# An expert's high and low rows stacked on 128 partitions for one combine product, and routing in one pass over five blocks of logits

## The chip, the cores and the metric

The kernel runs on one core of a Trainium2 chip. The metric is device time in microseconds (us). TensorE (PE) multiplies, VectorE (DVE), ScalarE (ACT) and GpSimd (POOL) work on elements, and SyncE (SP) issues most of the transfers between device memory and the on-chip memory of 128 partitions. PSUM is the memory of eight banks that TensorE writes to.

## The reference

One layer of a flow-matching backbone for 384 tokens (128 of context and 256 latent) of width 1024, in float32. The first half is a token mixer: modulation, an input projection, a bidirectional recurrence and a Fourier mixer, an output projection and a layer norm. The change lies in the second half, a hierarchical mixture of experts:

```python
pg = softmax(t @ wg + bg)                       # 4 expert groups
g = argmax(pg); p_top = pg[g]
le = (t @ we + be).reshape(ntok, 4, 4)          # 4 experts in each group
pe = softmax(le[g]); v, idx = top_k(pe, 2); v = v / sum(v)
w_k = p_top * v
eidx = g * 4 + idx
comb = sum(one_hot(eidx, 16) * w_k)             # 384 x 16
hid = silu(t @ w_gate[e]) * (t @ w_up[e]) * comb[:, e]
out = sum over e of hid @ w_down[e]             # each expert: 1024 -> 512 -> 1024
x = layer_norm(alpha * x + g2 * out)
```

Every token goes to two experts of one group, so there are 768 rows of work over 16 experts.

## The kernel before

Tokens lie in three tiles of 128 (`NT`). The routing turns the logits (`lg`, for each token 4 of groups, then 16 of experts) into marks and positions. `first_max` is a helper of five steps on VectorE. Each waits for the one before it (`link`), and together they take a maximum over the last axis, mark where it is reached, and reduce the marks to the first one. It runs over the group logits, then over the experts of each of the four groups, then once more with the first experts pushed down, for the second choice. Masks by the chosen group follow, then a scan that ranks the tokens. From the ranks TensorE computes each row's place among 768 slots, while VectorE makes the low part of tile 1 (`low_part(1)`) of the split tokens. `pick` and `pick2` mark the slots (`sel`), and the dispatch products (L1731) move the tokens' high and low parts (`h2H`, `h2L`) into slot order. Meanwhile come the gate weights (`comb`).

Then the experts run one after another, 48 weight units of 2 MB (gate, up and down for each of 16) streaming through a ring of seven buffers. SyncE issues unit v in order, and from the eighth on waits for unit v-7 to be used:

```python
                else:
                    sp.wait_ge(s["unit_used"], v - SLOTS + 1)
                sp.dma_start(weights(v, D if j == 2 else 512), experts[j][:, e]).then_inc(ring_in[v % SLOTS], 16)
```

Each engine's program is forked by the number of rows of the expert. `few` is for at most 64 rows (`HALF`) and `many` for up to 128. In this data experts 0 and 2 go through `many` and the others through `few`. With few rows the two 512-column halves of the expert's output lie on partitions 0 to 63 and 64 to 127 of one PSUM bank (L1830). ScalarE rounds this output to `yh` (`y_out`), VectorE subtracts to get the rest, `yl` (`y_low`), and TensorE multiplies both parts with the marks `selT` (`combine`), three times, once for each token tile. With few rows `selT` holds the same marks on both halves of the partitions. VectorE's `gather` weighs the product with the gate and adds it to the output (L1212).

TensorE's order is written out by hand. The combine of an expert is spread between the products of the next two:

```python
            for e in range(LAST - 1):
                project_in(e + 1, 0)
                if e:
                    combine(e - 1, 0)
...
                turn(e)
...
                project_in(e + 1, 1)
                if e:
                    combine(e - 1, 1)
...
                project_out(e)
                if e:
                    combine(e - 1, 2)
```

At e = 13 four `g2_row` products (L1925) that broadcast the last gate are put between these. After the loop come `turn(14)`, `combine(13, 0)`, `slot_weights` (L1915), `combine(13, 1)`, the output of expert 14, and the gate product of expert 15. Expert 15's output goes another way (`combine_last`), added to the residual that GpSimd (L1443, L1444) and VectorE (`settle`) prepare, and then the layer norm is taken.

Of the kernel before, what the change touches and what calls it, by code (L numbers as in the profile page):

```python
# [7 lines left out]
F32 = mybir.dt.float32  # L8
# [3 lines left out]
ALU = mybir.AluOpType  # L12
# [3 lines left out]
P = 128  # L16
# [5 lines left out]
NT = TOK // P  # L22
# [90 lines left out]
def build(nc, t):  # L113

    ctx = ExitStack()
    with ctx:
# [3 lines left out]
        def at(name, off, shape, dt=F32):  # L120
            return nc.alloc_sbuf_tensor_at(name, shape, dt, offset=off)
# [10 lines left out]
        def keep(name, shape, dt=F32):  # L132
# [36 lines left out]
        rt = keep("rt", [P, 8, NT, NE])  # L169
        stq = at("stq", place[0], [P, 24])  # L170
# [82 lines left out]
            "unit_used xs_ready sg_done silu_done hid_done ht_ps hts_done yh_done yl_done selA2 selT_done "  # L253
# [137 lines left out]
        def y_parts(e):  # L391
            return yh, yl
# [66 lines left out]
        def _(act):  # L459
# [200 lines left out]
            for n in range(2 * KD):  # L660
                if n == KD // 2:
                    act.wait_ge(s["prow_ps"], 1)
                    act.copy(Prow[:, :, :], PS[:, 0:2, 0:TOK]).then_inc(s["prow_sb"], 1)
                    act.wait_ge(s["x1_done"], NT)
                x_out(n)
                if n == KD + 1:
                    act.wait_ge(s["gap_done"], 1)
                    act.activation(rt[:, 6, :, 0:NG], rt[:, 5, :, 0:NG], ACT.Exp).then_inc(s["pos_pool"], 1)
                    act.activation(rs[:, 5, :], rs[:, 4, :], ACT.Exp).then_inc(s["pos_pool"], 1)
# [47 lines left out]
            def y_out(e):  # L717

                used(act, unit(e, 2))
                if e < LAST:  # L720
                    need(act, "c_ps", NT * e)
                need(act, "yl_done", e)
                if e == 0:
                    act.wait_ge(s["disp_sb"], 2 * KD)
                dst = y_parts(e)[0]
                fork(act, counts[e],
                     lambda: act.copy(dst[:, 0:512], PS[:, 3, :]).then_inc(s["yh_done"], 1),  # L727
                     lambda: act.copy(dst[:, :], PS[:, 3:5, :].rearrange("p a n -> p (a n)")).then_inc(s["yh_done"], 1))
# [49 lines left out]
        def _(dve):  # L778
# [277 lines left out]
            def by_group(v):  # L1056
                return v.rearrange("p i (g e) -> p i g e", e=EPG)

            og, oh1, oh2, asg = rt[:, 0, :, 0:NG], rt[:, 1], rt[:, 2], marks16[:, :, :]
            mx1, mx2, top = rt[:, 3, :, 0:NG], rt[:, 3, :, NG:2 * NG], rt[:, 3, :, 2 * NG:3 * NG]  # L1060
# [11 lines left out]
            link(dve.tensor_tensor_scan(rt[:, 7].rearrange("p i e -> p (i e)"), cst[:, C_SEG:C_SEG + NT * NE],  # L1072
                                        rt[:, 4].rearrange("p i e -> p (i e)"), 0.0, ALU.mult, ALU.add))
            dve.tensor_tensor(before16[:, :, :], rt[:, 7], rt[:, 4], ALU.subtract).then_inc(s["assign_done"], 1)
# [4 lines left out]
            place_ps = PS[:, 0, 0:NT * NE].rearrange("p (i e) -> p i e", e=NE)  # L1079
            step(dve.tensor_tensor(rt[:, 7], place_ps, oh1, ALU.mult))  # L1080
            step(dve.tensor_tensor(rt[:, 4], place_ps, oh2, ALU.mult))
# [3 lines left out]
            step(dve.tensor_reduce(pw[:, 1, :], rt[:, 4], AX.X, ALU.add))  # L1085
# [45 lines left out]
            step(dve.tensor_tensor(rt[:, 5, :, 0:NG], gl, wide(rs[:, 0, :], NG), ALU.subtract))  # L1131
            link(dve.tensor_tensor(rt[:, 4, :, 0:NG], mx2, mx1, ALU.subtract))
            link(dve.tensor_tensor(rt[:, 4, :, 0:NG], rt[:, 4, :, 0:NG], og, ALU.mult))
            link(dve.tensor_reduce(rs[:, 4, :], rt[:, 4, :, 0:NG], AX.X, ALU.add))
# [5 lines left out]
            link(dve.tensor_reduce(rs[:, 6, :], rt[:, 6, :, 0:NG], AX.X, ALU.add))  # L1140
            link(dve.tensor_scalar(rs[:, 7, :], rs[:, 5, :], 1.0, None, ALU.add))
            link(dve.tensor_tensor(rs[:, 6, :], rs[:, 6, :], rs[:, 7, :], ALU.mult))
            link(dve.reciprocal(wk[:, 0, :], rs[:, 6, :]))
            link(dve.tensor_tensor(wk[:, 1, :], wk[:, 0, :], rs[:, 5, :], ALU.mult))
            step(dve.tensor_tensor(rt[:, 3], oh1, wide(wk[:, 0, :], NE), ALU.mult))
            link(dve.tensor_tensor(rt[:, 4], oh2, wide(wk[:, 1, :], NE), ALU.mult))
            dve.tensor_tensor(comb[:, :, :], rt[:, 3], rt[:, 4], ALU.add).then_inc(s["comb_done"], 1)
# [46 lines left out]
            def y_low(e):  # L1194

                dve.wait_ge(s["yh_done"], e + 1)
                high, low = y_parts(e)
                fork(dve, counts[e],
                     lambda: dve.tensor_tensor(low[:, 0:512], PS[:, 3, :], high[:, 0:512].bitcast(F32), ALU.subtract)  # L1199
                     .then_inc(s["yl_done"], 1),  # L1200
                     lambda: dve.tensor_tensor(low[:, :], PS[:, 3:5, :].rearrange("p a n -> p (a n)"),
                                               high[:, :].bitcast(F32), ALU.subtract).then_inc(s["yl_done"], 1))
# [245 lines left out]
        def _(pe):  # L1448
# [368 lines left out]
            def project_out(e):  # L1817
# [3 lines left out]
                need(pe, "yh_done", e)  # L1821
# [21 lines left out]
            def combine(e, i):  # L1843

                if i == 0:
                    pe.wait_ge(s["yh_done"], e + 1)
                    pe.wait_ge(s["yl_done"], e + 1)
                    pe.wait_ge(s["selT_done"], e + 1)
# [6 lines left out]
                parts = y_parts(e)  # L1855

                def few():
                    for q, part in enumerate(parts):
                        for h in range(2):
                            mm = pe.matmul(PS[:, banks[h], :], m[HALF * h:HALF * (h + 1), i * P:(i + 1) * P],  # L1860
                                           part[HALF * h:HALF * (h + 1), 0:512], start=(q == 0), stop=(q == 1))
                    mm.then_inc(s["c_ps"], 1)

                def many():
                    for q, part in enumerate(parts):
# [168 lines left out]
```

## Time and profile before

| | us |
|---|---|
| median of 3 runs | 487.63 |
| lowest, highest | 487.33, 774.69 |
| profiled execution, its own time | 490.8 |
| its span | 488.6 |
| TensorE busy | 448.0 (92%) |
| VectorE busy | 236.4 (48%) |
| ScalarE busy | 121.7 (25%) |
| GpSimd busy | 63.3 (13%) |

The mean granted TensorE clock of that execution is 0.981 of full speed. It moved 146.90 MB, of which about 101 MB are expert weights. The span is from the first to the last instruction. The time is that of the whole execution, 2.2 us more. Busy time of one engine beside another is no cost in itself; what counts is which wait ends last at each place.

### The profile page before, as it was taken

How to read it: one execution, taken by the hardware profiler on the slowest of the kernel's cores; microseconds unless marked ns; L12 is line 12 of the kernel's file. 1: busy time of each engine (PE TensorE's matmuls, PEld its weight loads, DVE VectorE, ACT ScalarE, POOL GpSimd, SP SyncE). 2: the span in 40 equal slices, each digit the busy share in tenths (PEclk: the TensorE clock that was granted, in tenths of full speed). 3: DMA queues.
4: the chain of work that ended last, by engine and by line, in shares of the span. 5: the costliest groups of instructions: out<-in, count | busy, mean ns of one | idle time of the engine just before them, and what ended most of it. 6: DMA issues, size and time to landing. Idle time of an engine off the chain costs nothing.

```text
span 488.6 us, 6510 instructions
## 1 busy us (share of the span) xinstructions
PE 448.0 (92%) x2394; PEld 242.8 (50%) x2394; DVE 236.4 (48%) x446; ACT 121.7 (25%) x242; POOL 63.3 (13%) x61
## 2 busy tenths in 40 slices
PE   2679999999999999799999999999999999898882
PEld 1344455556554466696555444555554544363520
DVE  3552713848744257931024252444444445436767
ACT  2400168682220225162111111111111111121200
POOL 2000024357550430012000000000000000000300
PEclk9989999999999999799999999999999999999988
DMA  8999994855999026810899999999999999999403
GB/s 227 381 387 386 322 387 183 308 208 200 343 334 354 25 92 253 299 47 10 316 399 391 391 332 400 390 394 396 395 389 393 395 397 392 390 404 391 195 2 129
DMA packets 65380, 146.90 MB, mean 301 GB/s; under 512 B 3689, under 2 KB 4521, under 8 KB 65337
## 3 DMA queue, kind: packets, MB, share of 16 engines
q1 hardware_dynamic: 64144, 143.40, 80.1%
q10 hardware_dynamic: 1032, 2.81, 1.6%
q8 instruction: 29, 0.48, 0.4%
q0 software_dynamic: 160, 0.10, 0.3%
q14 instruction: 15, 0.11, 0.1%
HBM read 144.72 MB, written 1.58 MB: 299 GB/s over the span
## 4 chain that ended last, share of the span: by engine, by line
PE 71%; SPq 10%; DVE 6%; DMA 5%; issue 3%; ACT 2%; POOLq 1%; POOL 0%; DVEq 0%; ACTq 0%
PE PS L1790 18%; PE PS L1830 9%; PE PS L1656 8%; PE PS L1554 8%; PE PS L1797 6%; SPq L411 5%; PE PS L1860 4%; PE PS L1731 4%; DMA ring<-in_ex_w_gate 4%; SPq L416 2%; PE PS L1482 2%; PE PS L1531 2%; DMA dft<-in_dft 1%; PE PS L1837 1%; PE PS L1588 1%
## 5 line engine op out<-in xcount | busy, mean ns | idle before, releaser
L1790 PE MATMUL PS<-ring,xs 128*64 128x256 f32 x896 | 102.9, 382 | 2.3 <-DMA ring<-in_ex_w_gate 1.9
L1790 PEld LDWEIGHTS PS<-ring,xs 128*64 128x64 f32 x896 | 61.8, 137 | 39.3 <-issue 10.8
L1554 PE MATMUL PS<-hT,ring 128*128 128x388 f32 x192 | 67.5, 502 | 2.6 <-DVE hT L891 2.6
L1212 DVE SCALAR_TENSOR_TENSOR y<-PS,comb,y 128x1024 f32<-128x1024 f32 x42 | 53.6, 1278 | 0.4 <-PE PS L1867 0.3
L1554 PEld LDWEIGHTS PS<-hT,ring 128*128 128x128 f32 x192 | 36.7, 194 | 31.6 <-issue 8.3
L1830 PE MATMUL PS<-ring,hTs 128*64 128x512 f32 x224 | 51.2, 598 | 0.9 <-DMA ring<-in_ex_w_down 0.9
L1443 POOL TENSOR_TENSOR y<-y,g2r 128x1024 f32<-128x1024 f32 x1 | 2.4, 2362 | 236.1 <-DVE y L1212 236.1
L1830 PEld LDWEIGHTS PS<-ring,hTs 128*64 128x64 f32 x224 | 14.8, 136 | 30.9 <-issue 30.8
L727 ACT CAST yh<-PS 128x512 fp32r<-128x512 f32 x13 | 7.6, 586 | 88.9 <-PE PS L1830 56.7
L1199 DVE TENSOR_TENSOR yl<-PS,yh 128x512 fp32r<-128x512 f32 x13 | 9.0, 692 | 42.2 <-ACT yh L727 42.2
L1482 PE MATMUL PS<-ring,cond 128*32 128x512 f32 x192 | 25.0, 637 | 1.9 <-DVE cond L818 1.9
L1169 DVE SCALAR_TENSOR_TENSOR hid<-sg,PS 128x256 f32<-128x256 f32 x14 | 5.9, 421 | 37.8 <-PE PS L1790 37.8
L1656 PE MATMUL PS<-ring,yfs 128*128 128x512 f32 (+1 forms) x56 | 21.9, 533 | 0.0
L1656 PE MATMUL PS<-ring,mixT 128*128 128x512 f32 (+1 forms) x56 | 21.8, 531 | 0.0
L1400 POOL TENSOR_SCALAR gtmp<-gtmp 128x388 f32<-128x388 f32 x8 | 9.7, 1210 | 83.4 <-ACT gtmp L532 83.4
L1860 PE MATMUL PS<-yh,selT 64*128 64x512 f32 x78 | 19.3, 492 | 0.8 <-issue 0.8
L1731 PE MATMUL PS<-sel,h2H 128*128 128x384 f32 x48 | 18.1, 378 | 1.4 <-DVE sel L1100 1.4
L702 ACT ACTIVATE sg<-PS 128x256 f32<-128x256 f32 x14 | 5.4, 384 | 50.2 <-PE PS L1790 50.2
L1731 PE MATMUL PS<-sel,h2L 128*128 128x384 f32 x48 | 17.8, 370 | 0.0
L1860 PEld LDWEIGHTS PS<-yh,selT 64*128 64x128 f32 x78 | 7.3, 183 | 20.8 <-issue 20.7
L920 DVE TENSOR_SCALAR rtmp<-rtmp 128x388 f32<-128x388 f32 x8 | 6.2, 774 | 23.4 <-ACT rtmp L539 23.3
L1157 DVE SCALAR_TENSOR_TENSOR sg<-sg,PS 128x256 f32<-128x256 f32 x14 | 5.9, 422 | 21.8 <-ACT sg L702 21.8
(273 smaller groups left out, 606.1 us busy)
## 6 DMA issues: line engine op xcount, KB each, us to landing
ring<-in_ex_w_gate SPq DMA_DIRECT2D x16, 2048.0 KB, 14.1
ring<-in_ex_w_up SPq DMA_DIRECT2D x16, 2048.0 KB, 16.9
ring<-in_ex_w_down SPq DMA_DIRECT2D x16, 2048.0 KB, 15.0
ring<-in_w_ada SPq DMA_DIRECT2D x11, 2048.0 KB, 12.2
ring<-in_w_in SPq DMA_DIRECT2D x2, 2048.0 KB, 22.2
ring<-in_w_out SPq DMA_DIRECT2D x2, 2048.0 KB, 10.3
ring<-in_w_ada SPq DMA_DIRECT2D x2, 1024.0 KB, 15.2
ring<-in_w_in SPq DMA_DIRECT2D x2, 1024.0 KB, 14.7
```

The costliest lines, as they stand in the source:

```text
L411: sp.dma_start(dst[:, k0:, :], src[:, k0:, c0:c0 + 512]).then_inc(ring_in[(u + 1) % RING], 16)
L416: sp.dma_start(wbd[64 * h:64 * h + 64, 8 * gi:8 * gi + 8, 64 * h:64 * h + 64], t[n][0].rearrange("d (c q) i j -> q i (d c) j", q=2)[h]).th ...
L1212: dve.scalar_tensor_tensor(out=y, in0=src, scalar=comb[:, i, e:e + 1], in1=y, op0=ALU.mult, op1=ALU.add).then_inc(s["acc_done"], 1)
L1482: mm = pe.matmul(PS[32 * j:32 * j + 32, SUM_BANK[g], :], cond32[:, k, 6 - 2 * m:38 - 2 * m], w[:, k, :], start=(m == 0 and k < 4), stop=(l ...
L1531: mm = pe.matmul(PS[:, 4 + gi, 0:W], wbd[:, 8 * gi + 4 * d + c, :], xc[:, c, :], start=True, stop=True)
L1554: mm = pe.matmul(PS[:, w % 4, 0:W], wt[:, k, (w % 4) * P:(w % 4 + 1) * P], hT[:, k, :], start=(k == 0), stop=(k == KD - 1))
L1656: mm = pe.matmul(PS[:, bank, 0:nc_], x, unit3(ring[(WOUT_UNIT[h] + 1) % RING])[:, c, c0 % 512:c0 % 512 + nc_], start=(n == 0), stop=(n == ...
L1731: mm = pe.matmul(PS[:, 4 + n % 4, 0:HS], part[:, i, k * P:(k + 1) * P], sel[:, i, h * HS:(h + 1) * HS], start=(i == 0 and part is h2H), st ...
L1790: mm = pe.matmul(PS[HALF * h:HALF * (h + 1), bank, 0:FE // 2], x(k, HALF), w[:, k, h * (FE // 2):(h + 1) * (FE // 2)], start=(k == 0), sto ...
L1797: mm = pe.matmul(PS[:, bank, :], x(k, CAP), w[:, k, :], start=(k == 0), stop=(k == KD - 1))
L1830: mm = pe.matmul(PS[HALF * h:HALF * (h + 1), 3, :], x, w[:, f, h * 512:(h + 1) * 512], start=(f == 0), stop=(f == KF - 1))
L1860: mm = pe.matmul(PS[:, banks[h], :], m[HALF * h:HALF * (h + 1), i * P:(i + 1) * P], part[HALF * h:HALF * (h + 1), 0:512], start=(q == 0), ...
```

## The change

For an expert with at most 64 rows, the high parts of both output halves and their low parts go into one tile `yh` of 128 partitions by 1024. In the columns of half h, the high part stays on partitions 64h to 64h+63, and the low part goes to the other 64. ScalarE makes two copies of 64 partitions and VectorE two subtractions that read one half of the partitions and write the other. The combine product then takes the whole of `selT`'s 128 partitions, whose two halves are the same marks, and yields high plus low at once: two matmuls for each token tile where there were four. Nothing changes for an expert with more rows. The semaphore `yh_done` becomes `yh_part`, which counts two for each expert.

The routing runs `first_max` once over five blocks of four logits (the group block and the four expert blocks), and once over the four blocks for the second choice. The masks by the chosen group are applied to the sum of both marks first. Those of `oh1` and `oh2` alone come after the counts have been handed to TensorE. Tiles for the gate weights move, with the same number of steps.

```diff
-            first_max(gl, C_COD4, og, rs[:, 0, :], rt[:, 5, :, 0:NG], rs[:, 11, :])
-            x4, oh14, oh24, tmp4 = by_group(rt[:, 7]), by_group(oh1), by_group(oh2), by_group(rt[:, 4])
-            first_max(by_group(el), C_COD4, oh14, mx1, tmp4, top)
-            link(dve.scalar_tensor_tensor(out=rt[:, 7], in0=oh1, scalar=-2e30, in1=el, op0=ALU.mult, op1=ALU.add))
-            first_max(x4, C_COD4, oh24, mx2, tmp4, top)
+            first_max(by_group(lg[:, :, :]), C_COD4, by_group(oh5[:, :, :]), mx5, by_group(mark5[:, :, :]), top5[:, 1])
+            link(dve.scalar_tensor_tensor(out=rt[:, 7], in0=first, scalar=-2e30, in1=el, op0=ALU.mult, op1=ALU.add))
+            first_max(by_group(rt[:, 7]), C_COD4, by_group(oh2), mx2, by_group(rt[:, 4]), top)
             og4 = og.unsqueeze(3).broadcast_to([P, NT, NG, EPG])
-            step(dve.tensor_tensor(oh14, oh14, og4, ALU.mult))
-            link(dve.tensor_tensor(oh24, oh24, og4, ALU.mult))
-            dve.tensor_tensor(asg, oh1, oh2, ALU.add).then_inc(s["assign_done"], 1)
-            link(dve.tensor_tensor(rt[:, 4], oh1, oh2, ALU.add))
+            link(dve.tensor_tensor(pair, first, oh2, ALU.add))
+            dve.tensor_tensor(by_group(asg), by_group(pair), og4, ALU.mult).then_inc(s["assign_done"], 1)
+            link(dve.tensor_tensor(by_group(pair), by_group(pair), og4, ALU.mult))
...
+            step(dve.tensor_tensor(by_group(oh1), by_group(first), og4, ALU.mult))
+            step(dve.tensor_tensor(by_group(oh2), by_group(oh2), og4, ALU.mult))
             low_part(1)
...
+                def few():
+                    for h in range(2):
+                        act.copy(yh[half_rows(h), 512 * h:512 * (h + 1)], PS[half_rows(h), 3, :]).then_inc(s["yh_part"], 1)
...
+                def few():
+                    for h in range(2):
+                        dve.wait_ge(s["yh_part"], 2 * e + h + 1)
+                        low = dve.tensor_tensor(yh[half_rows(1 - h), 512 * h:512 * (h + 1)], PS[half_rows(h), 3, :],
+                                                yh[half_rows(h), 512 * h:512 * (h + 1)].bitcast(F32), ALU.subtract)
+                    low.then_inc(s["yl_done"], 1)
...
                 def few():
-                    for q, part in enumerate(parts):
-                        for h in range(2):
-                            mm = pe.matmul(PS[:, banks[h], :], m[HALF * h:HALF * (h + 1), i * P:(i + 1) * P],
-                                           part[HALF * h:HALF * (h + 1), 0:512], start=(q == 0), stop=(q == 1))
+                    for h in range(2):
+                        mm = pe.matmul(PS[:, banks[h], :], m[:, i * P:(i + 1) * P], yh[:, 512 * h:512 * (h + 1)],
+                                       start=True, stop=True)
                     mm.then_inc(s["c_ps"], 1)
```

## Rows read from the trace of the kernel before

**Rows 1.** The page, the span in 40 slices: transfer rate of each slice.

```profile
GB/s 227 381 387 386 322 387 183 308 208 200 343 334 354 25 92 253 299 47 10 316 399 391 391 332 400 390 394 396 395 389 393 395 397 392 390 404 391 195 2 129
```

**Rows 2.** Timeline of SyncE's queue, expert stage: start us, us, line, what.

```profile
230.42 0.37 SPq L432 DMA_DIRECT2D ring<-in_ex_w_down  x1
...
289.84 0.37 SPq L432 DMA_DIRECT2D ring<-in_ex_w_up  x1
...
368.47 5.32 SPq L432 DMA_DIRECT2D ring<-in_ex_w_down  x1
...
425.08 1.09 SPq L432 DMA_DIRECT2D ring<-in_ex_w_gate  x1
```

**Rows 3.** Timeline of TensorE, 420 to 457.5 us: the last wait for weights, expert 15.

```profile
426.59 3.67 PE L1790 MATMUL PS<-ring,xs 128*64 128x256 f32 x32 [0.93 <-DMA ring<-in_ex_w_gate]
...
452.40 3.67 PE L1790 MATMUL PS<-ring,xs 128*64 128x256 f32 x32
```

**Rows 4.** Transfer issues from 425 us to 426.1 us: KB, us to landing.

```profile
ring<-in_ex_w_gate SPq DMA_DIRECT2D x1, 2048.0 KB, 22.2
```

**Rows 5.** Timeline of VectorE, the routing: start us, us, line, what.

```profile
193.40 0.17 DVE L1046 TENSOR_REDUCE rs<-lg 128x3 f32<-128x12 f32 x1
...
194.42 0.20 DVE L1046 TENSOR_REDUCE rt<-lg 128x12 f32<-128x48 f32 x1
...
197.07 0.21 DVE L1067 TENSOR_TENSOR rt<-rt 128x48 f32<-128x48 f32 x1
...
197.79 0.26 DVE L1072 TENSOR_TENSOR_SCAN rt<-cst,rt 128x48 f32<-128x48 f32 x1
...
198.21 1.22 DVE L1020 TENSOR_TENSOR h2L<-PS,h2H 128x1024 fp32r<-128x1024 f32 x1
```

**Rows 6.** Timeline around the dispatch, and the chain's piece of its last 42.

```profile
201.55 0.66 PE L1731 MATMUL PS<-sel,h2H 128*128 128x384 f32 x1 [1.44 <-DVE sel L1100]
...
204.76 0.62 DVE L1100 SCALAR_TENSOR_TENSOR sel<-cst,pw,selA 128x384 fp32r<-128x384 f32 x1
...
208.57 1.50 PE L1746 MATMUL PS<-cst,pw 128*128 128x128 f32 x12
...
216.22 7.31 PE PS L1731 x42
```

**Rows 7.** Windows: us, busy of each engine, PEclk (granted clock), DMA share, GB/s.

```profile
202.00:204.00 2.00, 2.00 (x8) 2.00 (x8) 1.96 (x4) 0.00 (x0) 0.00 (x0) 0.50 0.90 294
```

**Rows 8.** Timeline of TensorE: a combine of expert 2 (many), two of expert 14.

```profile
311.97 0.73 PE L1867 MATMUL PS<-yh,selT 128*128 128x512 f32 x2
...
313.10 3.65 PE L1830 MATMUL PS<-ring,hTs 128*64 128x512 f32 x16
...
456.00 0.50 PE L1860 MATMUL PS<-yh,selT 64*128 64x512 f32 x2
456.34 0.39 PE L1860 MATMUL PS<-yl,selT 64*128 64x512 f32 x2
...
456.80 0.40 PE L1860 MATMUL PS<-yl,selT 64*128 64x512 f32 x2
457.13 3.67 PE L1790 MATMUL PS<-ring,xs 128*64 128x256 f32 x32
```

**Rows 9.** Timeline of all engines from 455 us: where the chain leaves TensorE.

```profile
456.93 0.42 DVE L1157 SCALAR_TENSOR_TENSOR sg<-sg,PS 128x256 f32<-128x256 f32 x1 [0.51 <-ACT sg L702]
...
458.73 2.36 POOL L1443 TENSOR_TENSOR y<-y,g2r 128x1024 f32<-128x1024 f32 x1 [236.06 <-DVE y L1212]
```

**Rows 10.** Timeline at expert 13's output: copy, subtraction, gather, combine.

```profile
443.76 0.59 ACT L727 CAST yh<-PS 128x512 fp32r<-128x512 f32 x1 [3.88 <-PE PS L1860]
...
444.59 0.69 DVE L1199 TENSOR_TENSOR yl<-PS,yh 128x512 fp32r<-128x512 f32 x1 [4.22 <-ACT yh L727]
...
445.20 1.27 DVE L1212 SCALAR_TENSOR_TENSOR y<-PS,comb,y 128x1024 f32<-128x1024 f32 x1
...
445.65 0.50 PE L1860 MATMUL PS<-yh,selT 64*128 64x512 f32 x2 [0.84 <-issue]
```

More of the change, by code:

```diff
@@ L169, in build @@
         rt = keep("rt", [P, 8, NT, NE])
+        oh5 = at("oh5", router0, [P, NT, NG + NE])
+        mark5 = at("mark5", router0 + 256, [P, NT, NG + NE])
+        top5 = at("top5", router0 + 512, [P, 2, NT, 5])
         stq = at("stq", place[0], [P, 24])
@@ L389, in halves, with half_rows @@
             return v.rearrange("p (a n) -> p a n", n=512)
-        def y_parts(e):
-            return yh, yl
+        def half_rows(h):
+            return slice(HALF * h, HALF * (h + 1))
         @block.sync
@@ L1064, in _ @@
-            link(dve.scalar_tensor_tensor(out=rt[:, 7], in0=oh1, scalar=-2e30, in1=el, op0=ALU.mult, op1=ALU.add))
-            first_max(x4, C_COD4, oh24, mx2, tmp4, top)
+            mx5 = top5[:, 0]
+            first_max(by_group(lg[:, :, :]), C_COD4, by_group(oh5[:, :, :]), mx5, by_group(mark5[:, :, :]), top5[:, 1])
+            mx0, mx1 = mx5[:, :, 0], mx5[:, :, 1:]
+            og, first = oh5[:, :, 0:NG], oh5[:, :, NG:]
+            oh1, oh2, pair, asg = rt[:, 4], rt[:, 5], rt[:, 6], marks16[:, :, :]
@@ L1084, in _ @@
             step(dve.tensor_reduce(pw[:, 0, :], rt[:, 7], AX.X, ALU.add))
-            step(dve.tensor_reduce(pw[:, 1, :], rt[:, 4], AX.X, ALU.add))
+            step(dve.tensor_reduce(pw[:, 1, :], rt[:, 6], AX.X, ALU.add))
             dve.wait_ge(s["dve_step"], n_step[0])
@@ L1129, in _ @@
                 dve.tensor_scalar(io[:, q, :], io[:, q, :], -1.0, None, ALU.add).then_inc(s["io_done"], 1)
[L1131 to L1134, printed above, removed]
+            gaps, over, gap = mark5[:, :, 0:NG], mark5[:, :, NG:2 * NG], rs[:, 8, :]
+            step(dve.tensor_tensor(over, gl, wide(mx0, NG), ALU.subtract))
+            link(dve.tensor_tensor(gaps, mx2, mx1, ALU.subtract))
+            link(dve.tensor_tensor(gaps, gaps, og, ALU.mult))
+            link(dve.tensor_reduce(gap, gaps, AX.X, ALU.add))
             dve.nop().then_inc(s["gap_done"], 1)
@@ L1139, in _ @@
             dve.wait_ge(s["pos_pool"], 2)
[L1140 to L1147, printed above, removed]
+            total, ratio = rs[:, 10, :], rs[:, 9, :]
+            link(dve.tensor_reduce(total, mark5[:, :, 2 * NG:3 * NG], AX.X, ALU.add))
+            link(dve.tensor_scalar(rs[:, 11, :], ratio, 1.0, None, ALU.add))
+            link(dve.tensor_tensor(total, total, rs[:, 11, :], ALU.mult))
+            link(dve.reciprocal(wk[:, 0, :], total))
+            link(dve.tensor_tensor(wk[:, 1, :], wk[:, 0, :], ratio, ALU.mult))
+            step(dve.tensor_tensor(rt[:, 6], oh1, wide(wk[:, 0, :], NE), ALU.mult))
+            link(dve.tensor_tensor(rt[:, 7], oh2, wide(wk[:, 1, :], NE), ALU.mult))
+            dve.tensor_tensor(comb[:, :, :], rt[:, 6], rt[:, 7], ALU.add).then_inc(s["comb_done"], 1)
             counts = {}
@@ L1194, in y_low, with many @@
             def y_low(e):
[L1196 to L1202, printed above, removed]
+                def few():
[4 more added lines that the diff above has]
+                    low.then_inc(s["yl_done"], 1)
+                def many():
+                    dve.wait_ge(s["yh_part"], 2 * e + 2)
+                    dve.tensor_tensor(yl[:, :], PS[:, 3:5, :].rearrange("p a n -> p (a n)"),
+                                      yh[:, :].bitcast(F32), ALU.subtract).then_inc(s["yl_done"], 1)
+                fork(dve, counts[e], few, many)
             def gather(e, i):
@@ L1820, in project_out @@
                 pe.wait_ge(s["hts_done"], e + 1)
-                need(pe, "yh_done", e)
+                need(pe, "yh_part", 2 * e)
                 need(pe, "yl_done", e)
@@ L1854, in combine @@
                 banks = c_banks(e, i)
-                parts = y_parts(e)
                 def few():
-                    for q, part in enumerate(parts):
-                        for h in range(2):
-                            mm = pe.matmul(PS[:, banks[h], :], m[HALF * h:HALF * (h + 1), i * P:(i + 1) * P],
-                                           part[HALF * h:HALF * (h + 1), 0:512], start=(q == 0), stop=(q == 1))
+                    for h in range(2):
+                        mm = pe.matmul(PS[:, banks[h], :], m[:, i * P:(i + 1) * P], yh[:, 512 * h:512 * (h + 1)],
+                                       start=True, stop=True)
                     mm.then_inc(s["c_ps"], 1)
                 def many():
-                    for q, part in enumerate(parts):
+                    for q, part in enumerate((yh, yl)):
                         for h in range(2):
```

25 lines of the change are left out of this document (12 added, 13 removed).

## The prediction

> **What bounds the kernel now.** I first read the clock and the transfer rate by slice, then SyncE's queue, then TensorE's order of work, and last the three places that the diff touches.
>
> The expert stage, from about 223 us to 460 us, has two bounds that take turns. The transfer rate stands near 390 to 400 GB/s in nearly every slice from 232 us on, after two slices at 47 and 10 [rows 1]. The quiet comes because all seven buffers hold weights. SyncE can issue a load only when TensorE gives one back, the first at 230.42 [rows 2]. At first TensorE sets the pace: SyncE's issues are short (0.37 us) at 230.42 and at 289.84. Later the loads do: an issue at 368.47 takes 5.32 us, for the queue behind it is full [rows 2]. At 426.59 TensorE, which has worked through its lead, waits 0.93 us for gate weights [rows 3]. After that it is the bound again. It also makes the broadcast rows of the last gate there, and gate weights issued at 425.08 land 22.2 us later, at 447.3, and are used at 452.40, with 5.1 us to spare [rows 2 to 4]. From there on the chain runs through TensorE's short products, at 457.3 through VectorE into GpSimd [rows 9], and on to the last layer norm.
>
> So time saved on TensorE between 290 us and 426 us becomes a longer wait for loads. Only two things move the end: an earlier start of the expert stage, which moves the whole stream of loads, and what happens after 426.59.
>
> **Part 1, the combine product.** An expert with at most 64 rows takes four matmuls of 64 rows by 512 columns for each token tile now, and two of 128 rows afterwards. Half the instructions looks like half the time, but the rows say otherwise. The two matmuls of a pair, one on partitions 0 to 63 and one on 64 to 127, occupy 0.50 us together at 456.00, while two full ones in a row take 0.73 at 311.97 [rows 8]. The halves of the array therefore work side by side. From 456.00 to 457.13 stand two combine steps, that is four such pairs, in 1.13 us. From 311.97 to 313.10 stand four full matmuls, and they also take 1.13 us [rows 8]. A pair costs what one full matmul costs. The new step has two full matmuls for two pairs. Its entry is 0.34 (456.00 to 456.34) and its exit 0.33 (456.80 to 457.13), so it takes 0.67 us, against 0.66 now [rows 8]. I take a saving of 0. One bound is the inner step: 456.34 to 456.80 is two pairs, 0.23 each [rows 8]. If the exit fell to that, the saving would be 0.10 a step, at six steps on the chain after 426.59 (experts 12 and 13, three tiles each) 0.6 us. The other bound is a loss of 0.01 a step.
>
> The Trainium skill has the rule that speaks against this half of the change. "TensorEngine Tiling (Array Packing)", section "Theoretical Speedup", gives up to twice the throughput to products whose dimension is at most 64, since the array then works as two tiles. By that rule the kernel before already has the factor of two that stacking seems to bring, and the sum would hold nothing for it. The trace agrees, with 0.50 us for a pair. Without that rule the sum would hold six times 0.33 us, which is the second case below.
>
> **Part 2, making the stacked rows.** One ScalarE copy of 128 partitions by 512 (0.59 us at 443.76) becomes two of 64 partitions, and one VectorE subtraction (0.69 us, but 0.61 to the next start: 444.59 to 445.20) becomes two, the second after the second copy [rows 10]. No row has a 64-partition copy of this kind. Between half and all of the old duration each, I take all, since the number of elements per partition stays 512. The second copy runs beside the first subtraction, so the pair adds one subtraction, 0.61 us, before the low part is ready (bounds 0 and 0.69).
>
> For experts 1 and 3 to 12 a whole input product of 3.6 us lies between the expert's output and its combine, and it covers this. If it didn't, the load queue would still hide it. For expert 13 nothing covers it: ScalarE at 443.76, VectorE at 444.59, TensorE's combine at 445.65 after 0.84 us idle [rows 10]. There all of 0.61 lands on the chain. Behind it TensorE has the slot weights and the next output product, and VectorE its gathers, and all move with it. Expert 14's low part feeds a combine that has room, but VectorE serves it in order ahead of expert 15's gate product, before which VectorE idles 0.51 us at 456.93 [rows 9]. Of the second 0.61 about 0.10 is left over, and GpSimd's step at 458.73 waits for VectorE's gather right behind [rows 9]. ScalarE's later copies of gate rows slip 0.5 us under the same 0.61. Sum of part 2: +0.7 us.
>
> **Part 3, routing.** VectorE works alone here. The pass over the group logits, 193.40 to 194.42, is five linked steps of 0.20 us and goes (-1.02). Its five blocks now ride in the expert pass. Twelve elements cost 0.20 a step and 48 cost 0.24 (194.42 to 197.07, eleven steps), so 60 cost about 0.25, +0.07 over five steps [rows 5]. The four masks and sums from 197.07 to 197.79 (0.72) become three (0.24 + 0.12 + 0.24 = 0.60): -0.12. Two unlinked masks are made before the low part of tile 1, which started at 198.21, +0.24 [rows 5]. Sum: -0.83 us until the positions are ready. TensorE's ranks, which need only the first three terms, start 1.07 us earlier and stay ahead of VectorE, so nothing new is late. The renamed tiles for the gate weights keep their number of steps and lie under the dispatch.
>
> Dispatch then starts at 200.7 instead of 201.55 [rows 6]. Not all of this arrives. TensorE's granted clock is at its low level (1.2 GHz, 0.50 in the row) from 202 to 204 [rows 7]; before 201.55 it had idled 1.44 us for the marks [rows 6]. The first 24 dispatch matmuls take 7.02 us (201.55 to 208.57), where 42 later ones take 7.31 in all, 0.174 each [rows 6]. If the low stretch ends at the same instant as now, work done 0.83 us earlier is done at half speed and gives 0.42. If it moves with the work, it gives all 0.83. No row decides, and I take 0.6. Whatever arrives moves the first returned buffer at 230.42 and the whole stream of loads, hence the wait at 426.59.
>
> **The sum.** The profiled execution took 490.8 us, with 2.2 us outside its span of 488.6. Combine 0.0, stacked rows +0.7, routing -0.6: 490.9 us for the same conditions. The median of the runs shown is 487.63, 3.2 us below the profiled execution, so I forecast 487.7.
>
> **The rivals.** (a) The sum holds: within about 1 us of before, 487.7. For it: equal times for four pairs and four full matmuls. (b) The combine does become half as long, because the overlap of a pair is less real than the recorded ends say: six steps of 0.33 us after 426.59, -2.0, so 485.7. Against it, the start of the next product after each step is recorded too, and it shows 0.66. (c) Dispatch runs at the high level, because TensorE's gap before the ranks closes. Then the marks of the third tile set the pace. Their second VectorE step starts at 204.76 and takes 0.62 [rows 6], so they come 0.83 us earlier, at 204.55, and eight matmuls of 0.174 end at 205.9 rather than 208.57. This gives 2.6 us at the start in place of 0.6, and 485.7. For it, the idle gap shrinks; against it, the gap right before dispatch (the marks' own) is left as it is. (d) Slower: the subtraction that reads one half of the partitions and writes the other costs twice as much. Nothing in the trace writes across halves. It is priced at one more 0.69 at expert 13 and one more at expert 14, +1.4, and it decides as soon as both late low parts are more than 0.5 us above my price. With routing giving only 0.42 it comes to 489.3. That the change saves nothing at all on TensorE is no case of its own, it is part of (a).
>
> **How the numbers follow.** (a) 0.70, (b) 0.06, (c) 0.14, (d) 0.10. The range takes in the bounds of (a) (combine -0.6, stacked rows 0 to 0.8, routing 0.4 to 0.8, so 486.0 to 488.1), (b) and (c) at 485.7, and (d) at 489.3. The profiled execution's distance of 3.2 us from the median says that a median can itself sit a us or two elsewhere, so the range is 484.7 to 489.7. Two per cent, about what a measurement of this kernel can tell from no change, is 9.8 us, further than any case reaches: faster 0.02, within 0.96, slower 0.02.
>
> **What would show it.** In the changed kernel two matmuls per combine step with the next product 0.66 us after the first, whereas 0.33 would prove (b). VectorE from the first maximum to the low part of tile 1 in 4.0 us instead of 4.8. Two subtractions of about 0.7 us per expert, and TensorE idle some 0.6 us longer before expert 13's combine. Waits for weights of the same or greater length up to 427 us, at a wall clock 0.4 to 0.8 us earlier. The prediction is wrong if the wait for loads disappears, if the dispatch shows another clock, or if cross-half subtractions are dearer.

## The result, and the profile after

The changed kernel takes 484.9 us (median of 20 runs, 482.19 to 490.3) beside 488.15 us for the kernel before (20 runs). The ratio is 0.9928, 95% interval 0.9909 to 0.9947: 0.7% faster, about 3.3 us. The prediction had 487.7 us and no net gain. Ratios, and the means below, leave out a run that is more than 1.5% above the fastest of its kernel (774.69 us before, 490.3 us here, 494.36 us in e10_cost). The profiled execution took 485.24 us, with a span of 483.4 us against 488.6.

VectorE's timeline of the routing in the changed kernel (start us, us, line, what), which answers to [rows 5]:

```profile
192.12 0.22 DVE L1054 TENSOR_REDUCE top<-lg 128x15 f32<-128x60 f32 x1
...
196.08 1.22 DVE L1028 TENSOR_TENSOR h2L<-PS,h2H 128x1024 fp32r<-128x1024 f32 x1
```

From the first maximum to the low part of tile 1 it takes 3.96 us (192.12 to 196.08), where [rows 5] had 4.81: 0.85 less. Everything around 190 us also stands 1.3 us earlier in this execution, before any changed line has run (the last logit product starts at 191.43 instead of 192.71). That is variation between executions and not the change.

TensorE's timeline at the dispatch, for [rows 6], and a window (PEclk is the third value from the end), for [rows 7]:

```profile
196.08 0.17 PE L1730 MATMUL PS<-marks,tri_ones 128*128 128x16 bf16 x1 [0.32 <-DVE before L1081]
...
199.43 0.41 PE L1750 MATMUL PS<-sel,h2H 128*128 128x384 f32 x1 [1.68 <-DVE sel L1110]
...
203.82 1.50 PE L1765 MATMUL PS<-cst,pw 128*128 128x128 f32 x12
```

```profile
200.00:203.00 3.00, 3.00 (x19) 2.83 (x18) 2.93 (x6) 0.00 (x0) 0.00 (x0) 1.00 1.05 401
```

The gap ahead of the rank products is 0.32 us. The first 24 dispatch matmuls take 4.39 us (199.43 to 203.82) instead of 7.02, because the granted clock is 1.00 (2.4 GHz) where [rows 7] had 0.50 (1.2 GHz). This is the largest single difference between the two traces, 2.6 us. It is a difference between two executions, and it doesn't say how often each level occurs: the experiments come back to that. The trace of before holds a second low stretch, at the first product of the residual, which the changed kernel's trace doesn't have (TensorE's timeline, before and then changed):

```profile
463.58 3.66 PE L1902 MATMUL PS<-y,cst 128*128 128x512 f32 x4 [1.35 <-POOL y L1444]
```

```profile
460.04 1.98 PE L1919 MATMUL PS<-y,cst 128*128 128x512 f32 x4 [1.37 <-POOL y L1463]
```

TensorE's timeline in the expert stage of the changed kernel, for [rows 3, 8]:

```profile
383.69 0.73 PE L1877 MATMUL PS<-yh,selT 128*128 128x512 f32 x2 [0.38 <-DVE y L1231]
384.26 0.38 PE L1831 MATMUL PS<-cst,hid 128*128 128x128 f32 x2
...
388.17 0.74 PE L1877 MATMUL PS<-yh,selT 128*128 128x512 f32 x2
388.84 3.65 PE L1849 MATMUL PS<-ring,hTs 128*64 128x512 f32 x16
...
421.46 3.67 PE L1809 MATMUL PS<-ring,xs 128*64 128x256 f32 x32 [1.05 <-DMA ring<-in_ex_w_gate]
```

A combine step of two full matmuls takes 0.67 us to the start of an output product (388.17 to 388.84), as predicted, but 0.57 before a transpose (383.69 to 384.26), where the old form takes 0.66. And there is a wait that the prediction didn't have: 0.38 us for VectorE's gather. The waits of TensorE between 215 and 440 us (us in total, times, longest), first of the kernel before and then of the changed one:

```profile
PE PS L1790 <- DMA ring<-in_ex_w_gate: 1.9, 2, 1.0
PE PS L1830 <- DMA ring<-in_ex_w_down: 0.9, 1, 0.9
...
PE PS L1790 <- DMA ring<-in_ex_w_up: 0.4, 1, 0.4
```

```profile
PE PS L1877 <- DVE y L1231: 3.5, 9, 0.4
PE PS L1809 <- DMA ring<-in_ex_w_gate: 1.1, 1, 1.1
```

TensorE used to wait 3.2 us for loads. Now it waits 1.1 us for loads and 3.5 for VectorE. Expert 13 in the changed kernel (copies, subtractions, combine), for [rows 10], with what follows, and a window there:

```profile
438.24 1.19 ACT L731 CAST yh<-PS 64x512 fp32r<-64x512 f32 x2 [3.87 <-PE PS L1877]
...
438.85 1.39 DVE L1212 TENSOR_TENSOR yh<-PS,yh 64x512 fp32r<-64x512 f32 x2 [3.80 <-ACT yh L731]
...
440.61 0.74 PE L1877 MATMUL PS<-yh,selT 128*128 128x512 f32 x2 [1.51 <-issue]
...
443.13 5.13 PE L1849 MATMUL PS<-ring,hTs 128*64 128x512 f32 x16
```

```profile
443.00:446.00 3.00, 3.00 (x9) 1.01 (x10) 2.93 (x6) 0.00 (x0) 0.00 (x0) 0.50 1.06 401
```

The two subtractions take 1.39 us and TensorE idles 1.51 instead of 0.84, +0.67. In this execution the clock then falls to its low level, and the output product takes 5.13 us instead of 3.65.

### The profile page after: what moved, and what is told of

Its sections match the earlier page's. It is cut to its first block, busy times and chain, and to the rows that moved or that the text cites. A ratio compares the mean times of both kernels' runs of the same rounds, so it can differ in the third digit from the quotient of the medians.

```text
span 483.4 us, 6377 instructions
## 1 busy us (share of the span) xinstructions
PE 442.2 (91%) x2316; PEld 240.7 (50%) x2316; DVE 246.0 (51%) x455; ACT 129.1 (27%) x255; POOL 63.9 (13%) x61
## 4 chain that ended last, share of the span: by engine, by line
PE 77%; DVE 9%; DMA 6%; issue 5%; ACT 2%; SPq 1%; POOLq 1%; POOL 0%; DVEq 0%; ACTq 0%
PE PS L1809 17%; PE PS L1573 12%; PE PS L1849 9%; PE PS L1675 9%; PE PS L1816 6%; PE PS L1501 4%; DMA ring<-in_ex_w_gate 4%; PE PS L1877 4%; PE PS L1750 4%; PE PS L1550 2%; PE PS L1856 1%; DMA pos<-in_pos 1%; PE PS L1607 1%; PE PS L1884 1%; PE PS L1592 1%
## 5 line engine op out<-in xcount | busy, mean ns | idle before, releaser
L1849 PE MATMUL PS<-ring,hTs 128*64 128x512 f32 x224 | 52.6, 613 | 0.3 <-issue 0.3
L731 ACT CAST yh<-PS 64x512 fp32r<-64x512 f32 x26 | 15.1, 581 | 89.1 <-PE PS L1849 61.5
L1212 DVE TENSOR_TENSOR yh<-PS,yh 64x512 fp32r<-64x512 f32 x26 | 17.9, 689 | 40.2 <-ACT yh L731 40.0
L1877 PE MATMUL PS<-yh,selT 128*128 128x512 f32 x78 | 29.2, 458 | 5.0 <-DVE y L1231 3.5
L1877 PEld LDWEIGHTS PS<-yh,selT 128*128 128x128 f32 x78 | 11.9, 188 | 24.7 <-issue 24.6
L1750 PE MATMUL PS<-sel,h2H 128*128 128x384 f32 x48 | 16.5, 343 | 1.7 <-DVE sel L1110 1.7
L1006 DVE TENSOR_TENSOR tmp<-PS,rows 128x512 f32<-128x512 f32 (+1 forms) x7 | 4.3, 616 | 24.3 <-PE PS L1675 24.3
L1750 PE MATMUL PS<-sel,h2L 128*128 128x384 f32 x48 | 16.1, 335 | 0.0
```

The lines of the kernel that those rows point to most:

```text
L731: act.copy(yh[half_rows(h), 512 * h:512 * (h + 1)], PS[half_rows(h), 3, :]).then_inc(s["yh_part"], 1)
L1212: low = dve.tensor_tensor(yh[half_rows(1 - h), 512 * h:512 * (h + 1)], PS[half_rows(h), 3, :], yh[half_rows(h), 512 * h:512 * (h + 1)].bit ...
L1750: mm = pe.matmul(PS[:, 4 + n % 4, 0:HS], part[:, i, k * P:(k + 1) * P], sel[:, i, h * HS:(h + 1) * HS], start=(i == 0 and part is h2H), st ...
L1849: mm = pe.matmul(PS[HALF * h:HALF * (h + 1), 3, :], x, w[:, f, h * 512:(h + 1) * 512], start=(f == 0), stop=(f == KF - 1))
```

## The experiments

Each ran beside the kernel before on the same chip, in three batches. The mean granted clock of every execution is on record, so each kernel has a mean time and a mean clock over its runs. Of the kernel before, the 87 runs taken beside the experiments average 488.3 us and 0.9834. Of the changed one, 31 (first result and e4) average 484.8 us and 0.987. A mean clock doesn't say where in a run the low stretches lie. In the traces they are found at three places behind 34 us and ahead of 470 us: the dispatch, expert 14's output, and the first product of the residual.

| label | ratio to before, 95% interval | mean us | mean clock |
|---|---|---|---|
| e1_routing | 0.9956, 0.9928 to 0.9985 | 486.6 | 0.9865 |
| e2_combine | 0.9984, 0.9957 to 1.0011 | 487.4 | 0.9826 |
| e3_fill | 1.0047, 1.0022 to 1.0073 | 490.4 | 0.9866 |
| e4_after | 0.9928, 0.9900 to 0.9956 | 484.6 | 0.9873 |
| e5_fill2 | 0.9987, 0.9964 to 1.0010 | 486.9 | 0.9873 |
| e6_full | 0.9984, 0.9955 to 1.0013 | 487.2 | 0.9829 |
| e7_mixed | 0.9929, 0.9903 to 0.9956 | 484.6 | 0.9857 |
| e8_double | 1.0104, 1.0073 to 1.0134 | 493.0 | 0.9872 |
| e9_late | 1.0003, 0.9974 to 1.0033 | 488.1 | 0.9810 |
| e10_cost | 1.0062, 1.0030 to 1.0095 | 490.5 | 0.9809 |
| e11_best | 0.9922, 0.9892 to 0.9952 | 483.5 | 0.9887 |

My theory A after the result: the gain is routing's, through VectorE's time and through the clock of the dispatch, and the stacked rows cost 0.7 us. The rival B: the combine's halved matmuls.

**e1_routing, the routing half alone** (the diff is the first block of the change shown above).

> Only the routing half of the change; the combine is that of the kernel before. Theory A (the gain is routing's: 0.8 us less on VectorE ahead of the dispatch, and a dispatch whose granted clock is more often high, worth another 1 to 2.6 us; the stacked rows cost 0.7 us at expert 13): 3 to 4.5 us faster than before, 0.7 us faster than the whole change. Theory B (the gain is the combine's, half the matmuls on the chain after the last wait for weights): 0.5 to 1 us faster than before, slower than the whole change by 2.5 us.

It is 0.4% faster, about 2 us: less than A said and more than B said. The first 24 dispatch matmuls run at the high clock in its trace, and its mean clock is near that of the changed kernel, 0.9865. The same trace has low stretches at expert 14's output and at the residual.

**e2_combine, the stacked rows alone** (the other blocks).

> Only the stacked rows and the combine of two matmuls; the routing is that of the kernel before. Theory A: 0.3 to 1 us slower than before, with TensorE idle about 1.5 us instead of 0.84 before expert 13's first combine, and dispatch at whatever clock the kernel before has. Theory B: 2 to 3 us faster than before.

Against A, it isn't slower: 0.16% faster, with an interval that reaches over 1. Its clock is that of the kernel before. So B's 2 to 3 us isn't there, and neither is A's loss. The halves add up to most of the whole (1.7 and 0.9 us in the means, 3.5 for the whole).

**e3_fill, TensorE's gaps filled in the kernel before.**

```diff
+                for _ in range(count):
+                    pe.matmul(PS[:, 5, 0:64], ident, cst[:, C_ID:C_ID + 64], start=True, stop=True)
+
             pe.wait_ge(s["tri_done"], 1)
+            pe.wait_ge(s["x1_done"], NT)
+            busy(12)
             pe.wait_ge(s["assign_done"], 2)
...
             ada_sums(11, range(KD // 2, KD))
+            busy(16)
```

> The kernel before, with 12 small matmuls in TensorE's gap ahead of the rank products and 16 in its gap ahead of the dispatch; their results are not used. Theory A says that these gaps bring the granted clock down for the dispatch: with them filled, the first 24 dispatch matmuls take about 4.4 to 5.2 us instead of 7.0, and the time is about 1.5 to 2 us below that of the kernel before wherever that one had the low clock. If the clock has another cause, or isn't what costs time, no change within 0.5 us.

The filling was too long. Each call is two matmuls in the trace and costs 0.22 us, so the dispatch began 3.6 us late, and the kernel is slower, not faster as expected. Yet its 24 matmuls took 4.25 us and its mean clock rose to 0.9866, above the 0.9834 of the kernel before. That points to the gaps as what brings the clock down.

**e4_after, the changed kernel again.**

> The whole changed kernel once more, for a second trace and beside its halves: 3 to 4 us faster than before. By theory A its runs fall into groups by mean granted clock, a low stretch at the dispatch and one at expert 14's output being there or not, about 1.6 us of time for each 3.4 us at the low level; by theory B the clock of a run and its time are unrelated.

The same ratio as at first. In both sets the runs with a clock of 0.989 or 0.990 have spans near 481.6 us, those at 0.985 and 0.986 near 483.8, and those at 0.978 and 0.979 486.1. In its trace neither the dispatch nor expert 14's output is at the low level.

**e5_fill2, the same filling with 4 and 5 calls.**

> The kernel before with fewer small matmuls in TensorE's two gaps, 4 ahead of the rank products and 5 ahead of the dispatch, about 0.9 and 1.1 us; their results are not used. Dispatch should start 8.8 to 9.0 us after the last logit product, as in the kernel before, not 12.4 us as with the longer filling. Theory A (TensorE's gaps bring the clock down for the dispatch, and that is part of what routing gains): mean granted clock 0.986 or more instead of 0.983, and 1 to 1.5 us faster than before. If the clock isn't what costs time: no change within 0.5 us.

TensorE's timeline of e5_fill2 at the dispatch:

```profile
198.44 1.33 PE L1710 MATMUL PS<-cst 128*128 128x64 f32 x10
200.03 0.41 PE L1739 MATMUL PS<-sel,h2H 128*128 128x384 f32 x1 [0.26 <-DVE sel L1100]
...
204.45 0.72 PE L1754 MATMUL PS<-cst,pw 128*128 128x128 f32 x5
```

The dispatch starts 8.83 us after the last logit product, as before (8.84), and takes 4.42 us, where the trace of before had 7.02. The mean clock is 0.9873, and none of 12 runs is at or below 0.983, where 46 of 87 runs of the kernel before are. So the filling does raise the clock. The gain in time isn't shown: the interval reaches over 1. The mean is 1.3 us below the mean of all runs of before, and the medians of this comparison are 487.2 and 487.78.

**e6_full, two full matmuls on the old tiles.**

```diff
-                    for q, part in enumerate(parts):
-                        for h in range(2):
-                            mm = pe.matmul(PS[:, banks[h], :], m[HALF * h:HALF * (h + 1), i * P:(i + 1) * P],
-                                           part[HALF * h:HALF * (h + 1), 0:512], start=(q == 0), stop=(q == 1))
+                    for h, part in enumerate(parts):
+                        mm = pe.matmul(PS[:, banks[h], :], m[:, i * P:(i + 1) * P], part[:, 0:512], start=True, stop=True)
```

> The kernel before in all but the combine of an expert with few rows: two matmuls over 128 partitions, one on the high and one on the low tile, in place of four over 64. The output halves are mixed up by it, and ScalarE's copy and VectorE's subtraction stay single; so it has TensorE's side of the stacked rows without their cost. Theory A: about 1.5 us faster than before (0.3 outside the span, about 1.2 from shorter changes between tile shapes, mostly before the loads set the pace), with 0.84 us idle at expert 13 as before. If a full matmul costs what a pair costs and nothing else counts, as the prediction had it: no change within 0.5 us.

The mean is 1.1 us below before at the same clock (0.9829 and 0.9834), though the interval of the ratio reaches over 1. Its trace shows where TensorE's side saves. TensorE's timeline around expert 2 (its products use the whole array), first e6_full, then the kernel before:

```profile
270.23 7.03 PE L1797 MATMUL PS<-ring,xs 128*128 128x512 f32 x16
276.70 0.79 PE L1859 MATMUL PS<-yh,selT 128*128 128x512 f32 x1
...
277.66 3.65 PE L1830 MATMUL PS<-ring,hTs 128*64 128x512 f32 x16
```

```profile
274.27 7.03 PE L1797 MATMUL PS<-ring,xs 128*128 128x512 f32 x16
281.23 0.49 PE L1860 MATMUL PS<-yh,selT 64*128 64x512 f32 x2
...
281.89 3.65 PE L1830 MATMUL PS<-ring,hTs 128*64 128x512 f32 x16
```

From the start of the 16 matmuls to the next product it is 7.43 us instead of 7.62. Full-array products stand before and behind the first combine matmul, so the array doesn't change from one tile shape to another and back. Where the neighbours are split by columns, nothing is saved (281.24 to 281.91 is 0.67). From the gate product of expert 14 to the slot weights it takes 19.77 us instead of 20.32. The part outside the span stays at 2.14 us, not 1.83 as I had expected.

This trace and that of e10_cost show one more thing. Both kernels have the old routing and the old gaps, and yet the dispatch runs at the high level. TensorE's timeline of e10_cost:

```profile
196.59 0.17 PE L1716 MATMUL PS<-marks,tri_ones 128*128 128x16 bf16 x1 [1.39 <-DVE before L1074]
...
199.71 0.41 PE L1736 MATMUL PS<-sel,h2H 128*128 128x384 f32 x1 [1.45 <-DVE sel L1100]
...
204.10 1.50 PE L1751 MATMUL PS<-cst,pw 128*128 128x128 f32 x12
```

The first 24 matmuls take 4.39 us here and 4.42 us in e6_full. So the old gaps don't always bring a low stretch, and a single trace can't show that closing them removes it. Over many runs the difference is plain: 66 of 122 runs with the old routing (before, e2, e6, e10) have a mean clock of 0.983 or less, but 9 of 61 with the new one (changed, e1, e7, e8) and 1 of 24 with the old one and filled gaps (e3, e5).

**e7_mixed, the changed kernel with experts 13 and 14 in the old form.**

```diff
+        APART = (LAST - 2, LAST - 1)
...
                 def few():
+                    if e in APART:
+                        act.copy(yh[:, 0:512], PS[:, 3, :]).then_inc(s["yh_part"], 2)
+                        return
```

and the same fork in `y_low` and `combine`.

> The changed kernel, but experts 13 and 14 in the form before (one copy, one subtraction, four matmuls of 64 rows). TensorE's idle time before expert 13's first combine falls from 1.5 to 0.84 us. Theory A: 0.3 to 0.7 us faster than the changed kernel, since the load stream no longer covers these two experts. If the stacking costs nothing at expert 13: the same as the changed kernel within 0.3 us.

The trace has the gain: from the last wait for loads to the slot weights it takes 19.57 us, where e4_after takes 20.26. In this trace the dispatch is in part at the low level, with the new routing. The time doesn't show it clearly: 484.6 us in the mean, at a clock of 0.9857 against 0.987.

**e8_double, the suspected cost doubled.**

```diff
                         dve.wait_ge(s["yh_part"], 2 * e + h + 1)
+                        if h == 0:
+                            dve.tensor_tensor(yl[half_rows(0), 0:512], PS[half_rows(0), 3, :],
+                                              yh[half_rows(0), 0:512].bitcast(F32), ALU.subtract)
```

> The changed kernel with one more VectorE subtraction of 64 partitions by 512 for each expert with few rows, into a tile that isn't used: the suspected cost doubled. Theory A (for 11 of 13 experts the load stream covers it, and only expert 13 and a little of 14 pay): 0.6 to 1.3 us slower than the changed kernel. If it were paid by every expert: about 8 us slower.

Here A fell. The kernel is 8 us slower than the changed one: every expert pays. The waits of TensorE from 215 to 440 us in e8_double:

```profile
PE PS L1880 <- DVE y L1234: 11.1, 10, 1.4
```

No wait for loads is left. VectorE's subtraction stands ahead of the last gather of the expert before, that gather frees the PSUM banks of TensorE's next combine, and TensorE arrives at expert 14's gate weights 5 us after they have landed. What I had taken for cover, the stream of loads, was 3.2 us in all in the kernel before, and 1.1 us of it was left in the changed kernel.

**e9_late, VectorE's time put back into the routing.**

```diff
+            for _ in range(4):
+                link(dve.tensor_tensor(pair, first, oh2, ALU.add))
             link(dve.tensor_tensor(pair, first, oh2, ALU.add))
```

> The changed kernel with four more linked VectorE steps of 0.24 us ahead of the sum of the marks: 0.97 us put back into the routing, which also reopens TensorE's gap ahead of the rank products from 0.3 to about 1.3 us. If the gap matters for the clock (theory A): mean granted clock back from 0.987 to about 0.983, a low stretch at the dispatch in many executions, and 1.6 to 2.4 us slower than the changed kernel. If only VectorE's time counts: 1.0 us slower, with the same clock.

TensorE's timeline of e9_late at the ranks and the dispatch, and a window:

```profile
197.55 0.17 PE L1732 MATMUL PS<-marks,tri_ones 128*128 128x16 bf16 x1 [1.29 <-DVE before L1083]
...
201.00 0.41 PE L1752 MATMUL PS<-sel,h2H 128*128 128x384 f32 x1 [1.78 <-DVE sel L1112]
...
206.84 1.39 PE L1767 MATMUL PS<-cst,pw 128*128 128x128 f32 x11
```

```profile
202.50:205.50 3.00, 3.00 (x11) 3.00 (x11) 2.89 (x7) 0.00 (x0) 0.00 (x0) 0.50 0.99 332
```

The four steps add 1.07 us up to the dispatch (9.07 us after the last logit product instead of 8.00) and cost 3.3 us in all. The gap is open again, the dispatch is in part at the low level and takes 5.84 us, and the mean clock is 0.9810. The whole gain of the change is lost by four small instructions. This is the clearest evidence that time on this path is worth more than itself. Its trace also has a low stretch at expert 14's output, so not all of the lower mean clock need be the dispatch's.

**e10_cost, the kernel before with 0.6 us more on VectorE's path**: one more subtraction of 64 partitions by 512 for each expert with few rows.

> The kernel before with one more VectorE subtraction of 64 partitions by 512 for each expert with few rows, into columns that aren't used: the cost of the stacked rows without TensorE's side of them. By what the doubled cost showed, VectorE's delay is passed on to TensorE's first combine of every expert (about 0.4 us each, 9 or more times), which the load stream covers only up to the 3.3 us that TensorE waited for loads in the kernel before; so here the waits for loads shrink to about nothing, and the time grows by 0.7 (expert 13) to 2.0 us. If the load stream still covered all of it: 0.6 us. If nothing were covered: 5 us.

It is 0.62% slower, 2.2 us in the mean, a little over my 0.7 to 2.0, at a lower clock (0.9809 and 0.9834), so part of the 2.2 us may be the clock's. In its trace TensorE has no wait for loads left and 3.9 us of waits for VectorE's gather. As in e8_double, the cost is passed on, and the first 3.2 us of it go into waits that were there anyway.

**e11_best, the mixed kernel with fillings** (5 calls ahead of the dispatch, 5 ahead of the last residual product, as in e3_fill).

> The mixed kernel (changed, with experts 13 and 14 in the old form) with 5 small unused matmuls in TensorE's gap ahead of the dispatch and 5 in its gap ahead of the last residual product, to keep the clock. Theory A: mean granted clock 0.989 or more, no low stretch between 34 and 470 us in its trace, 0.5 to 1.5 us faster than the changed kernel, 4 to 5 us faster than before. If the fillings only delay the products behind them: the changed kernel's time or up to 0.5 us more.

It is the fastest: median 483.74 us, ratio 0.9922 (0.9892 to 0.9952). In the six runs the mean clock is 0.9887 and none is below 0.986. Its span in the trace is 480.2 us, with no low stretch between 34 and 470 us. Its advantage over the changed kernel, about 1.3 us in the means, lies inside the two intervals.

## Why the prediction was wrong

The forecast was a net +0.1 us, and the kernel became 3.3 us faster. Two terms of the sum were too small: routing, where the clock was priced as if the low stretch stayed, and the combine, taken as 0. The measured 484.9 us lies just inside the stated range, but only through the us or so that was added for the scatter of medians: the lowest case stood at 485.7. (By its own terms case (a) reaches down to 486.2 us, and not 486.0.) Two of the prediction's own signs of being wrong came: the dispatch shows another clock in the trace, and the waits for loads shrank from 3.2 to 1.1 us.

**The combine's bound by time (right in the main).** A full matmul does cost what a pair costs, and 0.67 us to the output product came as said. Rival (b), 0.33 a step, is refuted by the traces: four full matmuls in a row take 1.12 us in the changed kernel (452.45 to 453.57), as four pairs took 1.13 before [rows 8]. The rule that the prediction quoted from the Trainium skill, "TensorEngine Tiling (Array Packing)", section "Theoretical Speedup", agrees with the traces: the old form had its factor of two. The possible saving of 0.10 a step, which I named as a bound and took as 0, is real wherever the neighbour has the full shape: before transposes, before the gate-row products (437.25 to 437.82 is 0.57), and around expert 2. After the last wait for loads these came to about 0.7 us, and cancelled the stacked rows' cost there: from the gate product of expert 14 to the slot weights it takes 20.27 us, against 20.32 before and 19.77 in e6_full. Ahead of 290 us, where TensorE sets the pace of the loads, it returns buffers up to 0.5 us earlier. I had read the saving only on the chain's end and forgot my own first finding, that the start of the stage is TensorE's too. This term of the sum was mis-sized: 0.0 stood for about -1.1. That is the difference of means of e6_full, whose interval still reaches over 1; its trace supports it, with 0.5 us by 290 us and 0.55 behind the last wait for loads.

**Stacked rows (size right, reason wrong).** Expert 13 cost 0.67 us, predicted 0.61 and a rest of 0.10. For experts 1 and 3 to 12 the sentence that failed is that the input product "covers this". The wait of a combine for the banks of the gather before it stood in the code, with a margin of about 0.2 us, and I priced only the wait for the low part. It costs 3.5 us over nine experts. It shows nothing in the time because TensorE had 3.2 us of waits for loads to give, and the shape changes saved some more. That "the load queue would still hide it" held by luck, since I had not added these waits up. e8_double and e10_cost show that once they are used up, nothing more is covered.

**Routing on VectorE (right).** -0.83 predicted; in the trace -0.85 up to the low part of tile 1 and -0.84 up to the dispatch.

**The clock at the dispatch (the step that failed).** "If the low stretch ends at the same instant as now ... gives 0.42. If it moves with the work, it gives all 0.83. I take 0.6." Both assumed that the low stretch stays. Rival (c) had the right mechanism, that the gap before the ranks closes, and got 0.14. Its price was too low as well. It waited for the VectorE step at 204.76, but by the loop over `pick` and `pick2` that is the first tile's mark for the second half of the slots. The first 24 matmuls need the third tile's mark for the first half, one step earlier in VectorE's timeline of before:

```profile
203.77 0.62 DVE L1100 SCALAR_TENSOR_TENSOR sel<-cst,pw,selA 128x384 fp32r<-128x384 f32 x1
```

With it (c) comes to 3.6 us at the start, and the two traces differ by 3.47 us from the last logit product to the end of these matmuls. But all of this compares executions that have the low stretch with executions that haven't, and the kernel before itself has both kinds. What the change shifts is how often. The gap goes from 1.40 to 0.32 us (the one behind it grows from 1.44 to 1.68). The dispatch has a low stretch in one of the five traces with the new routing as it is (e7_mixed), and in two of the four with the old one (before and e2_combine, not e6_full and e10_cost). That is too few to tell. The mean clocks over many runs do tell, though not of the dispatch alone: 0.9834 to 0.987, back to 0.9810 with the gap reopened (e9_late), up to 0.9873 with it filled (e5_fill2). Within one kernel the span changes by 300 to 460 us per unit of mean clock (the kernel before 487.6 us at 0.978 and 485.1 at 0.986; the changed one 486.1 at 0.979 and 481.5 at 0.989), so a rise of 0.0033 is worth 1.0 to 1.5 us, an estimate.

**The sum as measured.** VectorE -0.85, clock -1.0 to -1.5, TensorE's side of the combine -1.1, expert 13 +0.7, and -0.31 us outside the span (2.14 us in the kernel before, about 1.83 in every kernel with stacked rows). That is -2.6 to -3.1 us, against -3.3 (medians) to -3.5 (means) measured. The rest is within the intervals. The 0.31 us is open. It isn't the number of TensorE's matmuls, since e6_full has as few and keeps 2.14. The clock's worth was tested only with its cause, never alone at equal times on every engine, so its size remains an estimate.

The two traces shown differ by more, 5.2 us of span, and this can be placed. 1.28 us lie ahead of the changed lines, 0.84 are VectorE's, and 2.63 the dispatch's level: these make up the 4.75 us by which the first buffer comes back earlier (225.67 instead of 230.42). 0.38 us more are gained up to the last wait for loads and 0.05 up to the slot weights. Behind them the low stretch at expert 14's output in the one trace (+1.5) and that at the residual in the other (-1.7) about cancel.

## What to carry to other kernels

When two engines or an engine and a stream of transfers both look saturated, add up the waits of the one for the other: this sum, and not the length of the stage, is all that a new delay can hide in. Time saved ahead of a gap of TensorE can be worth more than itself: here the shorter gap made a low clock in what follows less frequent. Compare mean granted clocks over many runs before and after, since one trace shows only one draw, and before a forecast starts from a low stretch in a trace, ask whether the median run has it too. When packing products, look at the tile shape of their neighbours as well: here a pair and a full matmul cost the same, and the shape changes between products seem to have made about 1 us.

## What the runs showed of the hardware

A product of one tile shape behind another costs time of its own. At expert 2, the first combine matmul starts 0.52 us after the last matmul of the full-array product in the old form (before) and 0.03 us after it in the new one (changed), of which the first combine matmul then gives back 0.3. From the start of the last combine matmul to the next product it takes 0.33 us where the shape changes (before, 456.80 to 457.13), and 0.23 where it stays (e6_full, 285.85 to 286.08). Two subtractions of 64 partitions by 512 take 1.39 us together (0.69 each), as long each as one of 128 partitions (0.69), though they write the other half of the partitions than they read. The added subtraction of e10_cost, which reads and writes the same half, takes 0.68. So the split costs the whole of a second instruction, and crossing the halves costs next to nothing. The low level after expert 13 is in the changed kernel's first trace, in e9_late and in e8_double, but also in e1_routing with the old idle time of 0.84 us, and it is missing in e4_after and e2_combine with 1.51 us. So the same code meets it in some executions only, and I can't put it down to the stacked rows.
